# A transformer stack with a product-key expert layer on one Trainium2 core: the first two query units of the expert layer made for the first 128 tokens ahead of the other 128

## The reference, cut to what matters

```python
def peer_ffn(x, w_q, sub_keys, u, v):      # 8 heads, 128 keys per half, 16 picked
    ...
        q = (xb @ w_q).reshape(128, 8, 2, 128)
        scores = jnp.einsum('thpd,hpkd->thpk', q, sub_keys)
        top_s, top_i = lax.top_k(scores, 16)
        cand_s = top_s[:, :, 0, :, None] + top_s[:, :, 1, None, :]
        ...
        best_s, best_pos = lax.top_k(cand_s.reshape(128, 8, 256), 16)
        expert = jnp.take_along_axis(cand_i, best_pos, axis=-1)
        gate = jax.nn.softmax(best_s, axis=-1)
        act = gelu(jnp.einsum('thkd,td->thk', u[expert], xb))
        return jnp.einsum('thk,thkd->td', gate * act, v[expert])
```

## Time and profile before

| what | us |
|---|---|
| median of 3 runs | 1870.84 (1870.21 to 1872.37) |
| the profiled execution, its own time | 1869.32 |
| its span in the trace | 1867.5 |

### The profile page before, as it was taken

One profiled execution on the slowest core, in us unless ns is written; L12 is line 12 of the kernel. 1 busy time (PEld: TensorE's weight loads), 2 busy tenths in 40 slices (PEclk: granted clock), 3 DMA queues, 4 the chain that ended last, 5 costly groups with the idle time before them and its releaser, 6 DMA issues.

```text
span 1867.5 us, 29197 instructions
## 1 busy us (share of the span) xinstructions
PE 1738.5 (93%) x11150; PEld 1378.9 (74%) x11150; DVE 1274.3 (68%) x2524; ACT 910.5 (49%) x1905; POOL 320.8 (17%) x335
## 2 busy tenths in 40 slices
PE   9999999999999999999999999999987787877777
PEld 8999979999999999689999899975532222322222
DVE  6555787555765575876566887896777776766454
ACT  5344665444544453764444565635444444344433
POOL 1000004000000000030000000444333333333332
PEclk9999999999999999999999999999999999999999
DMA  8555426965465545225555444699999999999998
GB/s 300 190 183 188 146 85 161 271 251 187 158 201 184 187 154 184 80 93 188 195 175 176 150 137 137 222 406 422 421 421 422 421 421 422 421 421 422 421 422 318
DMA packets 96138, 483.70 MB, mean 259 GB/s; under 512 B 10576, under 2 KB 10832, under 8 KB 63360
## 3 DMA queue, kind: packets, MB, share of 16 engines
q0 software_dynamic: 38976, 275.25, 38.2%
q1 hardware_dynamic: 57024, 206.59, 32.9%
HBM read 477.34 MB, written 4.46 MB: 258 GB/s over the span
## 4 chain that ended last, share of the span: by engine, by line
PE 59%; DMA 16%; DVE 10%; issue 8%; POOL 4%; ACT 3%; POOLq 0%; SPq 0%; ACTq 0%; DVEq 0%
PE PS L562 15%; PE PS L564 15%; PE PS L563 15%; PE PS L2412 5%; DMA raw<-uv,A 5%; DMA WL<-uv,A 3%; DVE WL L1098 2%; DMA XL<-uv,A 2%; DMA A<-uv,A 2%; DMA raw<-wst 2%; PE PS L2448 1%; ACT WH L717 1%; DMA XF<-uv,A 1%; DMA YL<-uv,A 1%; POOL raw L695 1%
## 5 line engine op out<-in xcount | busy, mean ns | idle before, releaser
L1098 DVE TENSOR_TENSOR WL<-raw,WH 128x1024 fp32r<-128x1024 f32 (+2 forms) x372 | 447.9, 1245 | 76.8 <-ACT WH L717 76.5
L562 PE MATMUL PS<-XH,WH 128*128 128x256 f32 x1608 | 456.3, 284 | 4.7 <-DVE XL L1106 3.1
L563 PE MATMUL PS<-XL,WH 128*128 128x256 f32 x1608 | 452.5, 281 | 0.0
L564 PE MATMUL PS<-XH,WL 128*128 128x256 f32 x1608 | 452.4, 281 | 0.0
L717 ACT ACTIVATE WH<-raw 128x1024 fp32r<-128x1024 f32 (+2 forms) x372 | 369.2, 1042 | 41.0 <-PE PS L564 20.1
L562 PEld LDWEIGHTS PS<-XH,WH 128*128 128x128 f32 x1608 | 303.3, 189 | 9.3 <-DVE WL L1098 4.2
L563 PEld LDWEIGHTS PS<-XL,WH 128*128 128x128 f32 x1608 | 303.4, 189 | 0.1
L564 PEld LDWEIGHTS PS<-XH,WL 128*128 128x128 f32 x1608 | 303.3, 189 | 0.0
L1038 ACT ACTIVATE A<-A,RTK 128x1 f32<-128x1 f32 x256 | 74.9, 293 | 288.0 <-DVE A L1812 286.6
L772 ACT ACTIVATE A<-A 128x256 f32<-128x256 f32 x88 | 36.8, 418 | 342.7 <-DVE A L1140 342.7
L562 PE MATMUL PS<-GH,WH 128*128 128x256 f32 x704 | 198.3, 282 | 1.7 <-DVE WL L1098 1.1
(11 more groups left out here) (363 smaller groups left out, 2921.2 us busy)
## 6 DMA issues: line engine op xcount, KB each, us to landing
raw<-wst SPq DMA_DIRECT2D x378, 512.0 KB, 4.5
vscr<-A POOLq DMA_DIRECT2D x1, 3072.0 KB, 37.2
raw<-wst SPq DMA_DIRECT2D x6, 384.0 KB, 3.4
A<-vscr POOLq DMA_DIRECT2D x1, 2048.0 KB, 22.4
C<-cst SPq DMA_DIRECT2D x1, 1236.5 KB, 10.5
raw<-uv,A POOLq DMA_INDIRECT x66, 19.6
hT<-xin SPq DMA_DIRECT2D x2, 512.0 KB, 5.8
A<-vscr POOLq DMA_DIRECT2D x1, 1024.0 KB, 11.7
```

What stands on the lines that cost most here:

```text
L562: pe.matmul(o, wh, xh, start=start, stop=False, skip_group_check=True)
L563: pe.matmul(o, wh, xl, start=False, stop=False, skip_group_check=True)
L564: return pe.matmul(o, wl, xh, start=False, stop=stop, skip_group_check=True)
L1098: dv.tensor_tensor(WL[:, m % SPL, 0:w], raw[:, i % RAW, 0:w], f32(WH[:, m % SPL, 0:w]), ALU.subtract).then_inc(s_lo, 1)
```

## The change

For query units 0 and 1 the 24 matmuls over 256 tokens become 48 over 128 tokens: 24 for the first 128 tokens (block 0) and 24 for the others (block 1), each with its own load of weights (`block_of`). The order on PE becomes: unit 0 block 0; unit 1 block 0, its first six input blocks; the scores of unit 0 block 0; the other two input blocks; unit 0 block 1, six input blocks; the scores of unit 1 block 0; the other two input blocks; unit 1 block 1; the scores of units 0 and 1 for block 1. ACT copies the two blocks of these units apart. s_scm counts 1 and 2 at the scores of block 0 and 3 at those of block 1, and the waits of ACT on it go up by one.

```diff
@@ ACT, in the loop over query units n
                 if n == 0:
                     hi("pq", 1)
+                    for i in range(2):
+                        ac.wait_ge(s_part, 12 + i + 1)
+                        ac.activation(QP[:, i, 0:128], PS[:, bank_q[i], 0:128], ACT.Copy).then_inc(s_qn, 1)
                 ac.wait_ge(*queried(n))
                 if n >= QN_RING:
-                    ac.wait_ge(s_scm, (n - QN_RING) // 2 + 2)
-                ac.activation(QP[:, n % QN_RING, :], PS[:, bank_q[n], 0:T], ACT.Copy).then_inc(s_qp, 1)
+                    ac.wait_ge(s_scm, (n - QN_RING) // 2 + 3)
+                q = slice(128 if n < 2 else 0, 256)
+                ac.activation(QP[:, n % QN_RING, q], PS[:, bank_q[n], q], ACT.Copy).then_inc(s_qp, 1)
                 for h in scored(n):
-                    ac.wait_ge(s_scm, h + 2)
+                    ac.wait_ge(s_scm, h + 3)
@@ PE
+            def block_of(n, blk, k0, nk):
+                H, L = weights("pq", n)
+                q = slice(128 * blk, 128 * blk + 128)
+                for kc in range(k0, k0 + nk):
+                    if n == 0 and blk == 0:
+                        pe.wait_ge(s_xl, 56 + kc + 1)
+                    w = slice(128 * kc, 128 * kc + 128)
+                    ins = three(pe, PS[:, bank_q[n], q], H[:, w], L[:, w], YH[:, kc, q], YL[:, kc, q], kc == 0 and blk == 0, kc == 7)
+                return ins
-            def half_scores(h, i):
+            def half_scores(h, i, blks=(0, 1)):
-                pe.wait_ge(s_qp, 2 * h + 2 if h else i + 1)
-                for blk in range(2):
+                if h:
+                    pe.wait_ge(s_qp, 2 * h + 2)
+                elif blks[0] == 0:
+                    pe.wait_ge(s_qn, 8 + i + 1)
+                else:
+                    pe.wait_ge(s_qp, i + 1)
+                for blk in blks:
@@ PE, in the loop over query units n
+                if n == 0:
+                    block_of(0, 0, 0, 8).then_inc(s_part, 1)
+                    continue
                 if n == 1:
                     pe.wait_ge(s_sk, 16)
-                    gemm("pq", 1, 0, 4, Y, PS[:, bank_q[1], 0:T], last=False)
-                    half_scores(0, 0).then_inc(s_scm, 1)
-                    gemm("pq", 1, 512, 4, Y, PS[:, bank_q[1], 0:T], k0=4, first=False).then_inc(s_used, 1)
+                    block_of(1, 0, 0, 6)
+                    half_scores(0, 0, (0,)).then_inc(s_scm, 1)
+                    block_of(1, 0, 6, 2).then_inc(s_part, 1)
+                    block_of(0, 1, 0, 6)
+                    half_scores(0, 1, (0,)).then_inc(s_scm, 1)
+                    block_of(0, 1, 6, 2).then_inc(s_used, 1)
+                    block_of(1, 1, 0, 8).then_inc(s_used, 1)
+                    half_scores(0, 0, (1,))
                 elif n < SPLIT_PQ:
-                    gemm("pq", n, 0, 8, Y, PS[:, bank_q[n], 0:T], x=(s_xl, 56) if n == 0 else None).then_inc(s_used, 1)
+                    gemm("pq", n, 0, 8, Y, PS[:, bank_q[n], 0:T]).then_inc(s_used, 1)
...
-                    half_scores(h, 1).then_inc(s_scm, 1)
+                    half_scores(h, 1, (0, 1) if h else (1,)).then_inc(s_scm, 1)
```

## The result

The changed kernel takes 1873.7 us (median of 19 runs, 1872.0 to 1876.76) against 1870.74 of the kernel before measured beside it (19 runs): a ratio of 1.0016, 95% interval 1.0009 to 1.0022, or 3.0 us more (1.7 to 4.1). The time lies in the range of the prediction and within 0.2%, but the forecast was 0.6 us more. Most of the loss, then, is not in the sum.

What follows compares the result with a forecast made beforehand. Gathers at 422 GB/s bound the last stage, so the first gather's start and a never-empty queue set the end. First gather +0.47 and shallow queue +0.1 gave +0.6 us on 1870.84: 1871.4 us, range 1868.9 to 1874.6.

Steps and rivals of the forecast that it cites:

- the sum: Whole kernel: first gather +0.47 us and shallow queue +0.1 us, together +0.6 us on the 1870.84 us median.
- the path to the first gather: From unit 0 on PE through DVE's top 16 to POOL: first gather 0.47 us later, at 1213.0.
- The cost of a 128-column matmul: PE, query units 0 and 1: 0.110 us each, bound by the weight load, against 0.119 for 256 columns.
- The 81 ns of the Trainium skill: Figure behind the rival of better hidden loads on PE: 1.36 us gained, 1869.5 us, chance 0.10.
- slow fp32r: Rival on PE: 128-column fp32r matmuls cost the fp32 price, 0.22 us, giving 1881.5 us; chance 0.10.
- The second scores: PE, scores of unit 1 block 0: behind 66 matmuls, so DVE starts on them at 1207.20, 0.47 us later.
- Unit 2: PE, behind the scores of units 0 and 1: starts at 1211.60 against 1206.78, 4.8 us later.
- gather 16: Tightest gather waiting for PE: 4.7 us reserve against a lag of 4.3, so covered; issue near 1256.
- the shallow queue: DMA queue of gathers, shallow for a moment as PE lags: costs 0.1 us, from none to 1.0.
- the 1.5 us from an issue to its first traffic: DMA gathers: data follow an issue after about 1.5 us, subtracted from 6.2 us to give the 4.7 us reserve.
- the queue runs dry: Rival in the gather stage: the 4.8 us lag is passed on in full, 1875.6 us; chance 0.05.
- nothing falls below 415 GB/s: Gather stage, 1214 to 1300 us: no stretch clearly below 415 GB/s behind the start.

Runs made afterwards that it cites:

- fly2: The kernel before with at most two gathers in flight in the whole stage: 2008.92 us against 1870.62, ratio 1.074.
- fly3: The kernel before with at most three gathers in flight in the whole stage: 1911.18 us against 1870.92, ratio 1.0216.
- lag20: The kernel before with 20 extra 128-column matmuls, results unused, on PE behind the scores of unit 1: 1870.49 us against 1870.92, ratio 0.9999.

## Why the prediction was right, and where its size was off

The mechanism held on the path to the first gather. The cost of a 128-column matmul was taken as 0.110 us and is 0.1105: half the columns save 0.009 us. That the load is what bounds it fits this and the 0.107 us with two columns; it was not tested apart from another fixed cost of a matmul. The 81 ns of the Trainium skill (TensorE: Matmul & The Clock Gate, Back-to-back issue gap) is not reached by these fp32r pairs, and slow fp32r didn't come either. The second scores were put 0.47 us later and are 0.51 later. The first gather was put at 1213.0 if the stage ahead stood still; it moved by 0.51, and the gather came at 1212.54. Unit 2 was put 4.8 later; from the start of unit 0 it is 12.22 against 7.56, 4.7. Gather 4 was put at about 1223 (1222.30), gather 16 near 1256 (1255.47).

The term that was mis-sized is the shallow queue: 0.1 us was predicted, and b shows 3.5. The time lies in the range by luck: the range gave the queue 1.0 us at most, and 3.5 fitted only because the room left for a slower spacing and for the spread of the runs was not used. Two things in that step were wrong.

First, the price of a short lead. I took the 1.5 us from an issue to its first traffic as all that a gather has to lead by, so that a queue either holds or runs dry. fly2 and fly3 show a slope in place of an edge.

Second, only gather 16 was looked at, because of the gathers shown it was the one held by PE. Gather 10 comes ahead of it; it had waited for a landing and so looked safe. Its place was nearly as late, as PE's timeline of the kernel before shows for slots 1 and 10, and POOL's for gather 21, which waited for slot 9:

```profile
1234.20 1.88 PE L2412 MATMUL PS<-XL,A 128*128 128x512 f32 x4
...
1261.79 1.45 PE L2412 MATMUL PS<-XH,A 128*128 128x512 f32 x3
```

```profile
1262.72 0.95 POOL L695 DMA_INDIRECT WL<-uv,A  x1 [5.12 <-PE PS L2412]
```

PE was done with slot 9 when slot 10 began, at 1261.79, and gather 21 followed 0.93 later. By the same step gather 10, behind slot 0, could not have gone before 1234.20 + 0.93 = 1235.13; it went at 1235.70. So all but 0.6 us of a lag reaches the issue of gather 10: in the changed kernel it follows the first gather by 26.52 us in place of 23.16, 3.36 more at a lag of 3.93. Gather 5 had landed at 1233.21 - 0.30, gather 9 follows four gathers later, at 1242.85: a lead of 7.15 us before. After, it is 1232.74 + 9.94 = 1242.68 against the issue at 1239.06: 3.6 us, and the rate falls to 326 GB/s in the next stretch.

By its lead gather 16 was the tighter of the two before, 6.2 us in the prediction's reckoning against 7.15, and lag20 shows it: gather 10 has a lead of 5.2 us there and the rate holds, gather 16 has about 6.2 - 2.0 = 4.2 and the rate falls to 360. So the prediction had picked a tight place, though not the first. What failed is above all the price: a clear loss of rate begins at leads of 4 to 5 us, not at 1.5.

Of the rivals, "the queue runs dry" has the right place, but not its price: the lag is not passed on to the end of the query units. The rate is back at 426 GB/s from 1264, while units 11 to 15 are still ahead. The forecast that nothing falls below 415 GB/s was wrong.

## What to carry to other kernels

When an engine off the path is made later, list for every wait both what ended it and what would have ended it next; a wait that ends on a transfer can have a second condition less than a microsecond behind. A queue of transfers has to be judged by the rate it holds at a given depth, measured by setting the depth, and not by whether it is ever empty. What a lower rate costs is read from the stretches and from the end together, since the last transfers of a stage can give it back. And if fewer columns are to bring an answer forward, count the matmuls, each with its load: here one of 128 columns cost 0.1105 us and one of 256 cost 0.119.

## What the runs showed of the hardware

The DMA share hides a short queue. In the 24 us where the changed kernel moved 361 GB/s the share was 1.01, where the kernel before moved 420 it was 1.06; with two gathers in flight, from 1400 to 1600 us, it was 0.99 at 350 GB/s. The Trainium skill (Perfetto Trace Analysis, Identifying the Most-Contended Engine) says to judge DMA by the memory's rate and not by occupancy, since 16 engines make occupancy misleading; these traces agree, with a loss of 17% in rate at a share of 0.99. Why the engines are slower with fewer gathers of 128 rows in flight was not separated here: it was measured that they are, not by what.
